# Gathering an expert's row as two 4 KB halves, each into a buffer that its own reader gives back

## The reference, cut to what matters

```python
def peer(h, w_q, keys, u, v):
    def block(hb):                                   # 128 tokens
        q = (hb @ w_q).reshape(PEER_BLOCK, PEER_HEADS, 2, PEER_DQ // 2)
        s = jnp.einsum('thid,ikd->thik', q, keys).astype(jnp.float32)
        s1, i1 = lax.top_k(s[:, :, 0], PEER_TOPK)
        s2, i2 = lax.top_k(s[:, :, 1], PEER_TOPK)
        ...                                          # the 16 best pairs: expert ids e, scores sc
        g = jax.nn.softmax(sc, axis=-1)
        act = jax.nn.gelu(jnp.einsum('thkd,td->thk', u[e], hb)) * g
        return jnp.einsum('thk,thkd->td', act, v[e])
```

## Time and profile before

| what | value |
|---|---|
| time, median of 3 runs | 3838.04 us (3837.43 to 3840.01) |
| the profiled execution: its own time | 3826.18 us |
| the profiled execution: span | 3824.4 us |
| PE busy | 2769.3 us (72%) |
| DVE busy | 2117.8 us (55%) |
| POOL busy | 982.4 us (26%) |
| ACT busy | 728.1 us (19%) |
| transfers issued by POOL (queue q0) | 110592 packets, 805.36 MB |
| expert stage of layer 0 | from 918.58 to 1910.84 us |
| expert stage of layer 1 | from 2819.70 to 3810.87 us |

### The profile page before, as it was taken

One profiled execution on the slowest core, in us unless ns is written; L12 is line 12 of the kernel. 1 busy time (PEld: TensorE's weight loads), 2 busy tenths in 40 slices (PEclk: granted clock), 3 DMA queues, 4 the chain that ended last, 5 costly groups with the idle time before them and its releaser, 6 DMA issues. The chain is left out here.

```text
span 3824.4 us, 41999 instructions
## 1 busy us (share of the span) xinstructions
PE 2769.3 (72%) x15738; PEld 1366.1 (36%) x15738; DVE 2117.8 (55%) x5029; ACT 728.1 (19%) x1614; POOL 982.4 (26%) x868
## 2 busy tenths in 40 slices
PE   6999999997656544544479998999976565455453
PEld 3556755565111101111045567555751111011010
DVE  1316797126685677555413168971367756765554
ACT  1114311112222111111111142211122221111111
POOL 0000310002444444444300004000025444444442
PEclk9999899999888767766689998999988887677776
DMA  5221322233999999999852313314249999999997
GB/s 206 106 104 67 114 97 88 113 120 154 421 405 383 421 421 385 422 421 421 365 204 88 126 45 133 121 45 154 79 203 421 383 404 421 410 407 421 421 421 330
DMA packets 130764, 1001.17 MB, mean 262 GB/s; under 512 B 14960, under 2 KB 16304, under 8 KB 21500
## 3 DMA queue, kind: packets, MB, share of 16 engines
q0 software_dynamic: 110592, 805.36, 51.0%
q1 hardware_dynamic: 19968, 193.12, 13.4%
HBM read 994.51 MB, written 3.90 MB: 261 GB/s over the span
## 5 line engine op out<-in xcount | busy, mean ns | idle before, releaser
L1862 PE MATMUL bank<-arena 128*32 128x512 f32 x3072 | 579.4, 893 | 908.3 <-DVE arena L2021 908.3
L2012 DVE CUSTOM_DVE_ANT_0 arena<-arena 128x1024 f32<-128x1024 f32 x768 | 926.9, 1225 | 514.6 <-DMA arena<-in_experts_dram,arena 502.4
L1742 POOL DMA_INDIRECT arena<-in_experts_dram,arena x768 | 877.0, 1142 | 1245.0 <-PE bank L1862 887.9
L1862 PEld LDWEIGHTS bank<-arena 128*32 128x32 f32 x3072 | 102.9, 141 | 1327.5 <-DVE arena L2021 1082.9
L1780 ACT COPY arena<-bank 128x512 f32<-128x512 f32 x512 | 300.3, 587 | 451.0 <-PE bank L1845 439.1
L745 DVE SCALAR_TENSOR_TENSOR arena<-arena,vec 128x399 f32<-128x399 f32 (+1 forms) x576 | 322.3, 634 | 0.0
L795 PE MATMUL bank<-hT,arena 128*128 128x384 f32 x896 | 289.3, 486 | 0.0
L1562 PE MATMUL bank<-hT,arena 128*128 128x384 f32 x768 | 259.0, 491 | 0.0
L1786 ACT ACTIVATE arena<-arena 128x4 f32<-128x4 f32 x192 | 39.6, 206 | 1143.2 <-DVE arena L2012 1143.2
L1562 PE MATMUL bank<-arena 128*128 128x384 f32 x768 | 255.5, 486 | 0.0
L1845 PE MATMUL bank<-hn,consts 128*32 128x512 f32 x2048 | 244.4, 632 | 0.0
(11 more groups left out here) (251 smaller groups left out, 2980.3 us busy)
## 6 DMA issues: line engine op xcount, KB each, us to landing
arena<-in_w_big_dram SPq DMA_DIRECT2D x80, 2048.0 KB, 8.2
arena<-in_experts_dram,arena POOLq DMA_INDIRECT x768, 12.6
arena<-mod_scratch SPq DMA_DIRECT2D x8, 1024.0 KB, 11.2
arena<-in_w_uq_dram SPq DMA_DIRECT2D x6, 768.0 KB, 4.8
arena<-in_w_ukv_dram SPq DMA_DIRECT2D x2, 1024.0 KB, 4.8
arena<-in_h0T_dram SPq DMA_DIRECT2D x2, 1024.0 KB, 5.3
out_new_state_dram<-arena SPq DMA_DIRECT2D x8, 256.0 KB, 2.2
x<-in_x_dram SPq DMA_DIRECT2D x1, 1536.0 KB
```

The source lines that it names most:

```text
L1742: nc.gpsimd.indirect_dma_start(row(k), None, io["experts"], bass.IndirectOffsetOnAxis(ap=ei[:, t % 2, n:n + 1], axis=0))\
L1862: mm = nc.tensor.matmul(K.ps[ACC[c]][32 * a:32 * a + 32, :], Z[:, j % 2, a, 28 - 4 * r:60 - 4 * r], rw[:, D + c * 512:D + (c + 1) * 512], ...
L2012: nc.vector.tensor_tensor_reduce(out=U_rows, in0=U_rows, in1=spread_h[:, n_use % NH, :], scale=1.0, scalar=0.0, op0=ALU.mult, op1=ALU.add, ...
```

## The change

- The table is seen as 32,768 rows of 4 KB (`table`). Expert e's u half is row 2e, its v half row 2e + 1.
- Each gather of 128 rows of 8 KB becomes two gathers of 128 rows of 4 KB, into the two halves of the same buffer. POOL issues for each batch the four u halves, then the four v halves.
- The v halves have semaphores of their own (`gathered2`). The dot waits for its u half as before; PE waits before the v matmuls of a batch for the four v halves.
- A u half is refilled when the dot that read it is done (`dot_done`), a v half when the batch's matmuls are (`v_done`).
- `permuted` writes two index columns, 2e and 2e + 1: `tensor_scalar` with a multiply and an add, 16 in place of 8 copies for 64 or 128 columns. `ei` doubles, and `Z` moves to another place.

```diff
+        self.gathered2 = [nc.alloc_semaphore(f"second_{n}") for n in gather]
...
-    ei = K.at(o, 2, SLOTS).bitcast(U32)
-    Z = K.at(o + 256, 2, BATCH, 60)
+    ei = K.at(o, 4, SLOTS).bitcast(U32)
+    Z = K.at(o3_z(), 2, BATCH, 60)
...
+    table = io["experts"].rearrange("r (h n) -> (r h) n", h=2)
...
-                for n in range(SLOTS):
-                    g = base + t * SLOTS + n
-                    own = t * SLOTS + n
-                    k = g % ROWS
-                    if k >= 2 and own < ROWS:
-                        K.wait_full(pool, ("pq", 4 * (k // 2 - 1) + 3))
-                    if own >= ROWS:
-                        pool.wait_ge(S["v_done"], (own - ROWS) // BATCH + 1)
-                    nc.gpsimd.indirect_dma_start(row(k), None, io["experts"],
-                                                 bass.IndirectOffsetOnAxis(ap=ei[:, t % 2, n:n + 1], axis=0))\
-                        .then_inc(K.gathered[k], 16)
+                for b in range(NB):
+                    for half in range(2):
+                        for n in range(BATCH * b, BATCH * b + BATCH):
+                            g = base + t * SLOTS + n
+                            own = t * SLOTS + n
+                            k = g % ROWS
+                            if half == 0 and k >= 2 and own < ROWS:
+                                K.wait_full(pool, ("pq", 4 * (k // 2 - 1) + 3))
+                            if own >= ROWS:
+                                if half == 0:
+                                    pool.wait_ge(S["dot_done"], own - ROWS + 1)
+                                else:
+                                    pool.wait_ge(S["v_done"], (own - ROWS) // BATCH + 1)
+                            landed_at = (K.gathered2 if half else K.gathered)[k]
+                            nc.gpsimd.indirect_dma_start(row(k)[:, half * D:half * D + D], None, table,
+                                                         bass.IndirectOffsetOnAxis(ap=ei[:, 2 * (t % 2) + half, n:n + 1], axis=0))\
+                                .then_inc(landed_at, 16)
...
+                    for a in range(BATCH):
+                        g = base + t * SLOTS + BATCH * i + a
+                        pe.wait_ge(K.gathered2[g % ROWS], 16 * (g // ROWS + 1))
...
-                            dst = ei[:, t % 2, n:n + w].rearrange("p (r q a) -> p r q a", r=8, a=4)
-                            for r in range(8):
-                                steps(nc.vector.tensor_copy(dst[:, r], src[:, r]))
+                            for half in range(2):
+                                dst = ei[:, 2 * (t % 2) + half, n:n + w].rearrange("p (r q a) -> p r q a", r=8, a=4)
+                                for r in range(8):
+                                    steps(nc.vector.tensor_scalar(dst[:, r], src[:, r], 2.0, float(half), ALU.mult, ALU.add))
```

More of the change, by code:

```diff
@@ L1666, with o3_z @@
 B_ROUTE = CHUNK
+def o3_z():
+    return 26624 + 1044
 def experts(K, l):
```

## The result

The changed kernel takes 4368.76 us (median of 4 runs, 4340.49 to 4384.56) where the kernel before takes 3837.73 us beside it: 1.1375 times as long, interval 1.1315 to 1.1434. Slower was predicted, but 4018 and at most 4125.

A forecast was written before the change was run, and what follows sets the result against it. POOL's issue of gathers was to replace transfers as the bound: 1070 + 10.2 + 1.4 = 1082 us a stage for 992, two stages 180 more, 3826.2 to 4006, plus 11.9 gives 4018 us; range 3880 to 4125.

The forecast's parts named there:

- Order on POOL and PE: POOL's queue in the stages: v halves waiting for matmuls stand before u halves; priced at nothing, with some 19 us available.
- if POOL spends long in waits for dots or matmuls: Sign on POOL that the forecast is wrong, because the order of the queue would be the bound; no size given.
- the sum: Both expert stages: 1070 + 10.2 + 1.4 = 1082 us each for 992, 180 more in all, 4006 for the profiled execution.
- Twice as many gathers: POOL in the expert stages: a half costs a whole's 0.938 + 0.305 us; 11.15 us per batch, 1070 us a stage.
- the rhythm term: Gathers' wait behind dots on POOL, per batch: 0.6 us from below, 1.63 from above, middle 1.2 taken.
- the 1.04 to 1.14 us named: Sign in the changed profile: the gather line's mean time on POOL, with a median still near 938 ns.
- Rival 3: Expert stages: gathers and dots exclude each other both ways; a stage takes 181 us more, 4200 in all; chance 0.03.
- Rivals 1 and 2: Expert stages: transfers stay the bound, 3882 us or no change, chance 0.09; cheaper half gathers, closed gaps, 3790 us, chance 0.06.
- POOL is busy over 75% of the stages: Sign in the changed profile: POOL's busy share in the two expert stages, with POOL as the bound.
- 370 to 380 GB/s: Sign in the changed profile: the transfer rate in the expert stages falls to this from 421 GB/s.
- The early return of u halves: Buffers in the expert stages: worth nothing, since POOL arrives at each after its buffer is free.
- Smaller packets: Transfers of 4 KB rows: 4.6% more, 2.61 us a row instead of 2.49, hidden beneath POOL's 2.79 us.

## Why the prediction was wrong

**The step that failed** is "Order on POOL and PE": "So they are free in time, and the wait costs nothing", with "a few us in every fourth batch at most" if a spread came late. It set the v matmuls' end by a landing, the matmuls, and 5 to 7 us of spreads, all with durations of the kernel before, and found 19 us enough. In the changed kernel the copies of a spread come up to 17.5 us late. POOL then waits for matmuls: 299.7 us, and 367 with all waits inside the stages, priced at 0. The text named that sign ("if POOL spends long in waits for dots or matmuls"), but gave it no price and no chance, so the range had no room for it.

**The rest of the sum held.**
- Twice as many gathers: a half costs 937 ns in the median, a whole cost 938; 444.2 / 1453 is 0.306 us of issue behind each. A batch was put at 11.15 us and took 11.12, so the rhythm term's middle value came out. That is luck in part: the middle was taken because no row stood nearer to either end, and POOL's real rhythm has long waits in it that neither end assumed. The gather's mean, 1101 ns, lies inside the 1.04 to 1.14 us named.
- Without the 367 us the profiled execution would have been 3999 us, where the sum gave 4006. That is arithmetic; no run removed the waits without adding work to POOL.
- Rival 3 fell: dots are 1225 ns, as before. Rivals 1 and 2 fell with the rate, 313 to 322 GB/s, and with the median of 937 ns.
- "POOL is busy over 75% of the stages" and "370 to 380 GB/s" failed with the wait: 67%, and 313 to 322.
- The early return of u halves, priced at nothing, was worth some 100 us together with the new order, because buffers had become late for another reason.
- Smaller packets lay hidden, as said: with DMA 0.85 to 0.87 busy the transfers were not the bound.

**What caused the late copies** is shown as far as this: indirect gathers issued one close behind another, every 1.24 us, for long. Twice the gathers brings the lag with 64-byte and with 4 KB rows, with and without PE's waits; pauses between gathers take it away; as many plain transfers bring little of it (89 us), other work on POOL none (53 us). Why a stream of gathers does this to PE stays open. PE's counts come late, not ACT; but the trace models the ends of matmuls, so it can't tell whether PE's products ended late or only the word of their end came late. In 135 of the 159 late cases the next product had begun by the records before the count came, which speaks for the second and doesn't prove it.

## What to carry to other kernels

Before a transfer is cut in two, set the issue time of both against the time of the one: here 2 x 1.243 us of POOL stood against 2.49 us of transfer, and nothing was left over. A wait that is "free in time" should be priced also for the case that the waiting engine's new pace slows its releaser: the margin of 19 us held only as long as PE's word came at once, which the change itself altered. And where a wait is long, follow the chain back to the first late instruction: it was a copy on ACT, three engines away from the queue that had been changed.

## What the runs showed of the hardware that was not expected

- An indirect gather of 128 rows holds POOL for 0.94 us in the median, whether a row is 64 bytes, 4 KB or 8 KB. The next one follows 0.30 us later, a write on POOL at once.
- Long runs of gathers every 1.24 us make copies that wait for PE late, up to 17.5 us by the records, where they came 0.1 us behind PE. With gathers 1.39 us apart they are up to 3.7 us late; with 1.79 us, or in runs of four with a pause behind them, none is (longest 0.4).
- 768 tiny plain transfers beside the gathers cost 54 us: small transfers aren't free where the DMA engines are full (3.9% of their time for 0.95 of 122.77 MB, 1550 to 1850 us).
